# Experts' gate and up products as three single-pass products of rounded parts, with weights split one block ahead

## What is computed

```python
hg = jnp.einsum('nd,edf->nef', xt, w_gate)     # d = 1024, f = 128, e = 32
hu = jnp.einsum('nd,edf->nef', xt, w_up)
act = jax.nn.silu(hg) * hu * gates[:, :, None]
out = jnp.einsum('nef,efd->nd', act, w_down)
```

## Time and profile before

| | us |
|---|---|
| median of 3 runs | 685.01 |
| profiled execution, its own time | 688.35 |
| its span, first to last instruction | 686.5 |
| PE busy | 586.9 (85%) |
| PE weight loads (beside PE) | 501.9 (73%) |
| DVE busy | 369.6 (54%) |
| ACT busy | 204.2 (30%) |
| POOL busy | 98.5 (14%) |

### The profile page before, as it was taken

How to read it: one execution, slowest core, us unless ns; L and a number is a source line. 1 busy time by engine, 2 the same in 40 slices (tenths; PEclk the granted TensorE clock), 3 DMA queues, 4 the chain that set the end, 5 groups by cost and what they waited for, 6 DMA issues and landing times. The chain is left out here.

```text
span 686.5 us, 9515 instructions
## 1 busy us (share of the span) xinstructions
PE 586.9 (85%) x3131; PEld 501.9 (73%) x3131; DVE 369.6 (54%) x653; ACT 204.2 (30%) x351; POOL 98.5 (14%) x151
## 2 busy tenths in 40 slices
PE   3899999998998998999999629999999999997000
PEld 2899999977996896888887518777877777775000
DVE  4928988999695767376556760111111111111497
ACT  5632113220322354321221113332333233323232
POOL 4300002000000000000000221223323333232000
PEclk9999999998998999999999858999999999999555
DMA  9660111121103104463112477998999999940684
GB/s 318 126 139 11 52 32 31 51 62 32 32 8 124 61 3 136 185 215 139 63 61 77 134 260 236 291 314 313 310 352 322 330 341 324 308 175 24 265 351 167
DMA packets 51439, 116.27 MB, mean 169 GB/s; under 512 B 8434, under 2 KB 26743, under 8 KB 50295
## 3 DMA queue, kind: packets, MB, share of 16 engines
q1 hardware_dynamic: 42899, 92.82, 40.2%
q0 software_dynamic: 6656, 17.84, 7.7%
q10 hardware_dynamic: 1828, 4.96, 2.0%
HBM read 99.75 MB, written 20.68 MB: 175 GB/s over the span
## 5 line engine op out<-in xcount | busy, mean ns | idle before, releaser
L1659 PE MATMUL ps<-at_hT,at_ring 128*128 128x384 f32 x936 | 170.8, 340 | 3.6 <-DVE at_wk L1334 3.3
L1659 PEld LDWEIGHTS ps<-at_hT,at_ring 128*128 128x128 f32 x936 | 160.8, 193 | 9.2 <-issue 8.4
L1837 PE MATMUL ps<-at_hT,at_mring 128*128 128x512 f32 (+1 forms) x432 | 103.9, 397 | 3.5 <-DVE at_mring L1358 3.1
L1837 PEld LDWEIGHTS ps<-at_hT,at_mring 128*128 128x128 f32 (+1 forms) x432 | 78.5, 185 | 22.8 <-issue 4.1
L1538 DVE TENSOR_TENSOR at_actv<-at_sg,ps 128x128 f32<-128x128 f32 x35 | 10.1, 288 | 147.3 <-ACT at_sg L868 147.3
L1189 DVE SCALAR_TENSOR_TENSOR at_mixP<-at_uc,sb_par,at_mixP 128x1024 f32<-128x1024 f32 x60 | 77.4, 1289 | 2.1
L1929 PE MATMUL ps<-at_wlater,at_hTm 128*128 128x256 f32 x320 | 72.4, 379 | 0.0
L1929 PEld LDWEIGHTS ps<-at_wlater,at_hTm 128*128 128x128 f32 x320 | 59.2, 190 | 7.2
L1915 PEld LDWEIGHTS ps<-sb_ident,at_xg 128*128 128x128 f32 x280 | 37.5, 192 | 25.5 <-issue 23.6
L1929 PE MATMUL ps<-at_wfirst,at_hTm 128*128 128x256 f32 x240 | 55.8, 387 | 0.0
L1929 PEld LDWEIGHTS ps<-at_wfirst,at_hTm 128*128 128x128 f32 x240 | 45.6, 195 | 6.2 <-issue 0.3
(11 more groups left out here) (238 smaller groups left out, 657.2 us busy)
## 6 DMA issues: line engine op xcount, KB each, us to landing
at_wlater<-in_expert_w_gate SPq DMA_DIRECT2D x20, 512.0 KB, 5.7
at_wlater<-in_expert_w_up SPq DMA_DIRECT2D x20, 512.0 KB, 4.5
at_wlater<-in_expert_w_down SPq DMA_DIRECT2D x20, 512.0 KB, 5.9
at_raw<-in_w_in SPq DMA_DIRECT2D x16, 512.0 KB, 4.0
at_opair_p<-scratch_out SPq DMA_DIRECT2D x8, 1024.0 KB, 11.7
at_wfirst<-in_expert_w_gate SPq DMA_DIRECT2D x15, 512.0 KB, 5.4
at_wfirst<-in_expert_w_up SPq DMA_DIRECT2D x15, 512.0 KB, 4.9
at_wfirst<-in_expert_w_down SPq DMA_DIRECT2D x15, 512.0 KB, 6.2
```

What stands on the lines that cost most here:

```text
L1659: mm = pe.matmul(ps[:, bank + r, 0:t1 - t0], w[:, wpart, k * P:(k + 1) * P], hT[:, hpart, k, t0:t1], start=(m, wpart, hpart) == (0, 0, 0), ...
L1837: mm = pe.matmul(ps[0:n, b + r, :], mring[:, 1 - i % 2, mpart, k * P:k * P + n], wo[:, wpart, k, r * 512:(r + 1) * 512], start=(c, mpart, ...
```

## The change

In the expert stage, GU is computed from split operands, as the projections are:

- ACT's `expert_hT` writes `hTm` as float32r (the rounded high part; the semaphore is now `htm_hi`). DVE's new `expert_hT_lo` subtracts it from the PSUM value into `hTm_lo` (`htm_lo`), and T and GU wait for `htm_lo`.
- Gate and up weights of block j + 1 are split in two halves, of four of the eight 128-row parts each (1024 elements a partition). ACT's new `expert_whi` rounds half h into the buffer `whi[h]`, of which there is one for each half; it waits for the weights and, for half 0, for the first half of GU of the block before (`gu_half`), for half 1 for its end (`gu_done`). DVE's new `expert_wlo` subtracts `whi[h]` from the weights and writes the rest over them, in the weight slot.
- GU has 24 products of 256 columns in place of 8, and waits for `w_lo0` ahead of part 0 and for `w_lo1` ahead of part 4.
- The order in a step: on ACT hT (j+1), actT (j-1), whi0 (j+1), silu (j), whi1 (j+1), out (j-1). On DVE hT_lo (j+1), wlo0 (j+1), act (j), wlo1 (j+1), out (j-1).
- `wsT`, `wsb` and `pw`, which an earlier stage uses, move into a region `o_late` that `hTm_lo1` overlaps later. DVE's blocks 24 to 31 are written out.

The diff, cut to its core:

```diff
+        whi = [at("whi0", [P, 2, KC // 2, FF], o_raw + D * 2, F32R),
+               at("whi1", [P, 2, KC // 2, FF], o_sg + D * 4, F32R)]
...
-        hTm = at("hTm", [P, 2, KC, P], o_hTm)
+        hTm = at("hTm", [P, 2, KC, P], o_hTm, F32R)
+        hTm_lo = [at("hTm_lo0", [P, KC, P], o_w + 2 * D * 4, F32R),
+                  at("hTm_lo1", [P, KC, P], o_late, F32R)]
...
-                nc.scalar.activation(hTm[:, j % 2, :, :], src, ACT.Copy).then_inc(s["htm_ready"], 1)
+                nc.scalar.activation(hTm[:, j % 2, :, :], src, ACT.Copy).then_inc(s["htm_hi"], 1)
+
+            def expert_whi(i, j, h):
+
+                b = i * LAP + j
+                act.wait_ge(w_in_sem[j % LAP], 48 * lap(i, j) + 48)
+                if not (isinstance(b, int) and b < 1):
+                    act.wait_ge(s["gu_done" if h else "gu_half"], b)
+                nc.scalar.activation(whi[h][:], half(wexp(j), h), ACT.Copy).then_inc(s[f"w_hi{h}"], 1)
...
+            def ahead(i, j, last, work_on):
+
                 if not last:
-                    expert_hT(i, j + 1)
+                    work_on(i, j + 1)
...
+            def step(i, j, first, last):
+                ahead(i, j, last, expert_hT)
                 if not first:
                     expert_actT(i, j - 1)
+                ahead(i, j, last, whi0)
                 expert_silu(i, j)
+                ahead(i, j, last, whi1)
                 if not first:
                     expert_out(i, j - 1)
 
...
             act.wait_ge(s["o_done"], TILES)
+            whi1(0, 0)
+            act.wait_ge(s["idx_ready"], 2)
+            whi0(0, 0)
             expert_hT(0, 0)
...
+            def expert_hT_lo(i, j):
+
+                b = i * LAP + j
+                dve.wait_ge(s["htm_hi"], b + 1)
+                if not (isinstance(b, int) and b < 2):
+                    dve.wait_ge(s["gu_done"], b - 1)
+                src = ps[:, 0:2, :].rearrange("p b (k t) -> p (b k) t", t=P)
+                v.tensor_tensor(hTm_lo[j % 2][:], src, hTm[:, j % 2, :, :].bitcast(F32),
+                                ALU.subtract).then_inc(s["htm_lo"], 1)
+
+            def expert_wlo(i, j, h):
+
+                b = i * LAP + j
+                dve.wait_ge(s[f"w_hi{h}"], b + 1)
+                v.tensor_tensor(half(wexp_lo(j), h), half(wexp(j), h), whi[h][:].bitcast(F32),
+                                ALU.subtract).then_inc(s[f"w_lo{h}"], 1)
...
+            def step(i, j, first, last):
+                ahead(i, j, last, expert_hT_lo)
+                ahead(i, j, last, wlo0)
                 expert_act(i, j)
+                ahead(i, j, last, wlo1)
                 if not first:
                     expert_out(i, j - 1)
 
+            wlo1(0, 0)
+            wlo0(0, 0)
+            expert_hT_lo(0, 0)
...
-                    pe.wait_ge(s["htm_ready"], b)
+                    pe.wait_ge(s["htm_lo"], b)
...
-                pe.wait_ge(s["htm_ready"], b + 1)
+                pe.wait_ge(s["htm_lo"], b + 1)
                 if not early(b, 2):
                     pe.wait_ge(s["act_ready"], b - 1)
-                pe.wait_ge(w_in_sem[j % LAP], 48 * lap(i, j) + 48)
-                w = wexp(j)[:, 0:2 * D].rearrange("p (g k f) -> p g k f", g=2, k=KC)
+                out = ps[:, 2 + j % 2, 0:2 * FF].rearrange("p (g f) -> p g f", g=2)
                 for k in range(KC):
-                    mm = pe.matmul(ps[:, 2 + j % 2, 0:2 * FF].rearrange("p (g f) -> p g f", g=2),
-                                   hTm[:, j % 2, k, :], w[:, :, k, :], start=k == 0, stop=k == KC - 1)
-                mm.then_inc(s["gu_done"], 1)
+                    h = k // 4
+                    if k % 4 == 0:
+                        pe.wait_ge(s[f"w_lo{h}"], b + 1)
+                    high, low = whi[h][:, :, k % 4, :], half(wexp_lo(j), h)[:, :, k % 4, :]
+                    x, x_low = hTm[:, j % 2, k, :], hTm_lo[j % 2][:, k, :]
+                    pe.matmul(out, x, high, start=k == 0, stop=False)
+                    pe.matmul(out, x, low, start=False, stop=False)
+                    mm = pe.matmul(out, x_low, high, start=False, stop=k == KC - 1)
+                    if k % 4 == 3:
+                        mm.then_inc(s["gu_done" if h else "gu_half"], 1)
```

More of the change, by code:

```diff
@@ L133, in build_layer @@
         o_uc = o_w + 3 * WL * 4
-        o_end = o_uc + 2 * CL * 4
+        o_late = o_uc + 2 * CL * 4 + 16
+        o_end = o_late + D * 4
         lo, _ = nc.bump_sbuf(o_end)
@@ L151, in wexp, with half, wexp_lo @@
             return wfirst[:, j, :] if j < FIRST else wlater[:, j - FIRST, :]
+        wfirst_lo = at("wfirst_lo", [P, FIRST, 3 * D], o_x1, F32R)
+        wlater_lo = at("wlater_lo", [P, LAP - FIRST, 3 * D], o_hT, F32R)
+        whi = [at("whi0", [P, 2, KC // 2, FF], o_raw + D * 2, F32R),
+               at("whi1", [P, 2, KC // 2, FF], o_sg + D * 4, F32R)]
+        def half(x, h):
+            return x[:, 0:2 * D].rearrange("p (g k f) -> p g k f", g=2, k=KC)[:, :, h * 4:h * 4 + 4, :]
+        def wexp_lo(j):
+            j %= LAP
+            return wfirst_lo[:, j, :] if j < FIRST else wlater_lo[:, j - FIRST, :]
         xg = at("xg", [P, XG, D], o_xg)
@@ L213, in build_layer @@
         gain = sb("gain", [P, D])
-        wsT = sb("wsT", [P, NG, P])
-        wsb = sb("wsb", [NS, NG, NS])
-        pw = sb("pw", [P, 2, P])
+        wsT = at("wsT", [P, NG, P], o_late)
+        wsb = at("wsb", [NS, NG, NS], o_late + NG * P * 4)
+        pw = at("pw", [P, 2, P], o_late + NG * (P + NS) * 4)
         rw = sb("rw", [P, KC, 8 + NE])
@@ L287, in build_layer @@
             "ones_ready", "place_ready", "table_added", "cols_ready", "idx_ready", "ov_ready", "xg_zero",
-            "xt_done", "htm_ready", "gu_done", "sg_ready", "act_ready", "at_done", "att_ready",
+            "xt_done", "htm_hi", "htm_lo", "w_hi0", "w_hi1", "w_lo0", "w_lo1", "gu_half", "gu_done", "sg_ready", "act_ready", "at_done", "att_ready",
             "d_done", "ob_act", "ob_dve", "moe_done", "y_sum", "y_root", "y_done", "y_out")}
@@ L886, in expert_out, with whi0, whi1 @@
                     .then_inc(s["ob_act"], 1)
-            def step(i, j, first, last):
+            def ahead(i, j, last, work_on):
                 if not last:
-                    expert_hT(i, j + 1)
+                    work_on(i, j + 1)
                 else:
                     with act.If(total > 0):
-                        expert_hT(i, j + 1)
+                        work_on(i, j + 1)
+            def whi0(i, j):
+                expert_whi(i, j, 0)
+            def whi1(i, j):
+                expert_whi(i, j, 1)
+            def step(i, j, first, last):
+                ahead(i, j, last, expert_hT)
                 if not first:
                     expert_actT(i, j - 1)
+                ahead(i, j, last, whi0)
                 expert_silu(i, j)
+                ahead(i, j, last, whi1)
                 if not first:
@@ L921, in _ @@
                             expert_actT(i + NE // LAP, j - 1)
+                            with act.If(i * LAP + j + 1 < total):
+                                whi0(i + NE // LAP, j + 1)
                             expert_silu(i + NE // LAP, j)
+                            with act.If(i * LAP + j + 1 < total):
+                                whi1(i + NE // LAP, j + 1)
                             expert_out(i + NE // LAP, j - 1)
@@ L1546, in expert_out, with ahead, wlo0, wlo1 @@
                 v.tensor_copy(outb[:, j % 2, 512:D], ps[:, 6, :]).then_inc(s["ob_dve"], 1)
-            def step(i, j, first):
+            def expert_hT_lo(i, j):
[11 more added lines that the diff above has]
+                                ALU.subtract).then_inc(s[f"w_lo{h}"], 1)
+            def ahead(i, j, last, work_on):
+                if not last:
+                    work_on(i, j + 1)
+                else:
+                    with dve.If(total > 0):
+                        work_on(i, j + 1)
+            def wlo0(i, j):
+                expert_wlo(i, j, 0)
+            def wlo1(i, j):
+                expert_wlo(i, j, 1)
+            def step(i, j, first, last):
+                ahead(i, j, last, expert_hT_lo)
+                ahead(i, j, last, wlo0)
                 expert_act(i, j)
+                ahead(i, j, last, wlo1)
                 if not first:
                     expert_out(i, j - 1)
+            wlo1(0, 0)
+            wlo0(0, 0)
+            expert_hT_lo(0, 0)
             for j in range(LAP):
-                step(0, j, first=j == 0)
-            with dve.Fori(1, NE // LAP) as i:
+                step(0, j, first=j == 0, last=False)
+            with dve.Fori(1, NE // LAP - 1) as i:
                 for j in range(LAP):
-                    step(i, j, first=False)
+                    step(i, j, first=False, last=False)
             total = dve.value_load(ovt[0:1, 2 * OVER:2 * OVER + 1], min_val=0, max_val=OVER)
+            for j in range(LAP):
+                step(NE // LAP - 1, j, first=False, last=j == LAP - 1)
             with dve.If(total < 1):
```

(5 more changed lines are left out.)

## The result

The changed kernel takes 681.24 us (median of 5 runs, 678.86 to 682.09) against 685.01 us. The ratio is 0.9941, with a 95% interval of 0.9920 to 0.9962: faster by 4.0 us (2.6 to 5.5). A second series of 12 runs beside the kernel before gave 0.9949 (0.9924 to 0.9974); one of the 12, at 687.7 us, counts as slow and is not in the ratio. Lines 1090 and 1105 are now the gathers and scatters, 2003 the transposes T, 2021 to 2023 the three products of GU, 2043 the down products D, 886 the rounding of weights, 1606 their subtraction and 1590 DVE's outb copy.

What follows compares the result with a forecast made beforehand. PE was taken to bound the expert stage, with the gather loop nearly as long. Products -20.4, start +2.0, gather stalls +12.6, longer landings +1.6 sum to -4.2 us: 680.8 from 685.01, rounded to 680.5, range 668 to 691.

Steps and rivals of the forecast that it cites:

- The products: Gate and up products on PE: 24 at 0.119 us, 2.86 in place of 3.46 us a step; 20.4 us gained.
- The start: Start of the expert stage: DVE's subtractions ahead of block 1's transposes add 2.0 us.
- The stalls: PE's waits for late gathers: 3.3 us in the early stretch, 9.3 later, and 1.6 for longer landings.
- The idle time before T: Sign: PE idle before the transposes, waiting for gathers, 10 to 18 us in all, mostly after 513 us.
- The DMA share: Sign that the forecast is right: DMA engines busy at a share of 0.95 and more.
- the gathers take back what the products give: Forecast case in the expert stage: gather stalls of 5 to 17 us against 20.4 gained; chance 0.48.
- The third rival: Weights bound the expert stage, wanted one step earlier: at most some 8 us, shared with gather stalls; no separate chance.
- The allowance: Time for a gather to land in two PE steps: 6.60 us, or 6.1 with POOL held.
- POOL held: DVE subtractions with two SBUF inputs delay POOL's gathers: bounds 0 and 1.23 us each, taken as 0.5.
- Landings that grow with the load: Gathers land later as the early stretch wants 327 GB/s: 6.7 us at most, a quarter taken, 1.6.
- The slower rival: Gather loop becomes the bound everywhere, POOL held the full 1.23 us: 25.9 us of stalls, 692.5 us; chance 0.27.
- The first rival: PE stays the expert stage's bound, gathers keep pace as weight loads give way: 666.6 us; chance 0.12.

Runs made afterwards that it cites:

- v2: Changed kernel with gathers issued one block earlier and the up piece waiting for weights of the block two before, not one: 665.5 us, ratio 0.9719.
- e3: Changed kernel with a looser weight gate: the up piece waits for the weights of the block two before, not one: 680.0 us, ratio 0.9945.
- r_after: The changed kernel run and profiled again, unaltered: 682.2 us, ratio 0.9949.
- e2: Changed kernel with each gather issued one block earlier, ahead of the scatter, giving it three steps to land: 676.5 us, ratio 0.9898.
- e4: Changed kernel with the second input of both weight subtractions read from PSUM instead of SBUF, leaving out the weights' rests: 677.6 us, ratio 0.9901.
- e5: Changed kernel without the third product (rest of activations times high weights), 16 products a step: 680.9 us, ratio 0.9934.

## Why the prediction was right, step by step

The forecast was 680.5 us and the result is 681.24. Not all of the steps were right; some errors made up for others.

**The products: right.** 24 products at 0.118 us give 2.83 us (2.86 in the prediction, from the earlier trace rows), and PE's step is 5.53 (5.57). The v piece of the same kernel was the right place to read the price.

**The start: right.** From the start of T(0) to that of the first D it is 421.38 - 405.09 = 16.3 us in place of 423.04 - 408.62 = 14.4: 1.9 us, where the prediction has 2.0. ACT's table load for silu, now behind whi0, has a share in it that I hadn't seen.

**The stalls: right in sum, too simple in kind, and in the wrong place in part.** The prediction gives the gathers 12.6 + 1.6 = 14.2 us. The changed kernel's stage is 217.8 - 203.5 = 14.3 us over v2's (12.2 by the second profile), in which neither loop stalls for more than 1 us; by the timed ratios it is 15.2 us. In e3, where ACT never waits for weights, the stage is 217.4 - 203.5 = 13.9 us over v2's, so the gathers alone can take that much.

Where they take it is another matter. From the start of the first D to that of the 29th, the changed kernel needs 164.3 us and v2 154.9: 9.4 us, where the prediction has all 14.2 (7.8 in r_after, 10.9 in e3). The six steps behind that hold 35.3 - 30.6 = 4.7 us (5.0 in r_after). There I had put none, "with idle DMA engines", but T waited 2.6 us for the gathers of the extra blocks, and 3.9 in r_after. In r_after a wait of 3.55 us among these was followed by a granted clock of 0.74 from 604 to 608 us (its products stood 0.21 us apart to about 606, at 1.2 GHz, and 0.12 behind that), and the step took 10.94 us in place of 5.5. So the sum holds with one term too large and another left out, which is luck. The idle time before T that I had named as a sign, 10 to 18 us, reads 9.7 and 8.9: just under it. The DMA share, which I had put at 0.95 and more, is 0.85 to 0.94.

And the step "the gathers take back what the products give" names one of two. With the gathers' share removed (e2) only 3 us came out, since weights stood behind. The third rival had them, at "at most some 8 us of the same 18". e2's stage is 210.4 - 203.5 = 6.9 us over v2's, but by the timed runs e2 is 0.9898 - 0.9719 behind v2, 12.3 us, so that rival's price was too low, and its place, shared with the gathers, right. In the changed kernel ACT's waits for weights show in one profile and not in the other. That two loops at nearly the same length take turns may also be why its runs spread over 676.2 to 684.4 us (11 of 12) while v2's five lie within 663.1 to 666.6; that is argued, not shown.

**The allowance: two errors that cancel.** I read the gather's start, 3.40 us after D, from one step. The median in the same trace is 3.82. And I moved DVE's copy by 1.0 us, where it moved by 0.59. The sum, 4.40, meets 4.46 by luck.

**POOL held: the mechanism right, the place wrong.** The earlier trace rows carried over: two SBUF inputs lengthen the gather instruction by 0.34 us. It doesn't move its start, where I had put 0.5. The Trainium skill, "SBUF — State Buffer", section "Who interferes with whom", says that a DVE instruction with two SBUF inputs contends with a GpSimd instruction that reads SBUF. e4 agrees: the gather instruction reads its indices from SBUF, and it took 1322 against 979 ns. The page's inference that tensor_tensor spares descriptor generation e4 can't judge, since it has only the time of the instruction as a whole.

**Landings that grow with the load: the ceiling was wrong.** I called 327 GB/s "near the 334 of the busy one" and took that for the ceiling. It was the gate's doing. With AHEAD = 2 the engines moved 357 to 371. Whether the landings of the changed kernel grew, no view gives. The slower rival (692.5) needed all 27 gathers late at the lengths of the later stretch and their start held by 1.23 us. The start was not held, and the steps up to the 29th D lost 9.4 us, not 25.9.

**The first rival was a price and no case.** 666.6 us for "PE stays the bound" is near what v2 measures, 665.5; only it took two more edits to get there.

## What to carry to other kernels

When an engine's step gets shorter, list every loop that closes through other queues (buffer free, DMA issue, landing, use) with its own length, and compare them all with the new step. Of the two here one was at its limit in the old trace already, the other had no wait to its name, and removing either alone showed little. Prefetch one block deeper with the buffers already there, and a gate on loads set for the new pace, cost no memory and no work and were worth four times the change itself. Try such edits together before judging either alone. And where a test run leaves TensorE idle for longer, look at its granted clock before the idle time is read as the whole price.

## What the runs showed of the hardware that was not expected

- From 500 to 560 us the DMA engines moved 329 to 348 GB/s at a share of 0.94 to 0.98 in the eight kernels with one block's loads in flight behind the gate, and 357 to 371 at 1.00 to 1.02 in the six with two. A share of 0.95 was not full.
- A GpSimd indirect gather took 0.98 us beside DVE subtractions with one SBUF input and 1.32 beside the same with two; its start, behind index reads and branches, did not move.
- Waits of a few us before the transposes were followed by a lower granted clock in the expert stage: 0.94 and 0.97 in e5's two stretches, 0.74 in 604 to 608 us of r_after, where the changed kernel's undisturbed stretches have 1.00.
